# Keys and queries of a sparse-attention layer: projected by weights or by tokens

## The chip, the cores and the metric

The kernel runs on one core of a Trainium2 chip. The metric is the device time of one execution in microseconds; the lower the better. TensorE (PE) does matrix products into PSUM, VectorE (DVE), ScalarE (ACT) and GpSimd (POOL) do elementwise work, and SyncE (SP) issues the weight loads. Each engine carries out its own instructions strictly in the order in which they are written; semaphores tie the engines together.

## The reference, cut to what matters

A two-layer decoder trunk over 256 tokens of width 2048 in fp32. Layer 0 is stick-breaking attention and a gated MLP with a causal convolution. Layer 1 is a sparse attention, and again such an MLP. In layer 1 one weight matrix gives, per token, 16 query heads, 4 key heads, 4 value heads (each 128 wide) and an indexer whose top-k picks 64 keys per query:

```python
q = _rope(_rmsnorm(q, q_norm_g), cos, sin)      # 16 heads of 128
k = _rope(_rmsnorm(k, k_norm_g), cos, sin)      # 4 heads of 128
...
s = einsum(q, k of the selected positions) * attn_scale
p = softmax(s);  o = einsum(p, v);  x = x + o @ w_o
```

The norm is over the 128 values of a head; the rotation pairs value j with value j + 64. Four query heads share one key head and one value head.

## The kernel before, in words

**Weights.** All weights come as 771 "pieces" of 128 x 1024 fp32 through a ring of four buffers. For each piece SyncE loads `raw` (L240 to L251) as soon as VectorE is done with the piece four before it; ScalarE's `split` (L282, its instruction is L289) waits until PE has used the piece four before it (`piece_used`), and rounds the piece to `w_hi`; VectorE's `split` (L737, L747) forms `w_lo = raw - w_hi`. PE waits for `lo_ready`. Every other job of ScalarE and VectorE is written between the splits of certain pieces: the functions run over a slot number `e`, one per piece, and a job "at e" stands before or after the split of piece `e + 4`. This hand-written order is all that sets who does what when.

**Products.** The activations lie transposed as `xg[:, k, 0:256]` (high part) and `xg[:, k, 256:512]` (low part). `proj` (L1303) keeps a 128 x 128 tile of the weights stationary and streams activations: per tile one matmul of 512 columns with `w_hi` and one of 256 with `w_lo`, 16 matmuls and 6144 columns per piece; the result is channel by token, the high and low sums side by side. `proj_tokens` (L1352) keeps a 128 x 128 tile of the activations stationary and streams 512 weight columns: three matmuls of 512 columns for each of two row tiles and two token halves, 12 matmuls and 6144 columns per piece; the result is token by channel. Value heads already use it, as does the last product of layer 1 (with `hid` for `xg`).

**The stage of the change** is layer 1 after the value heads: blocks 9 and 10 (keys, two heads each, pieces `L1_K`), then blocks 11 to 18 (queries, two heads, a "pair", each, pieces `L1_Q`), four pieces a block, 40 pieces in all, then the output product `out_groups(BASE_WO[1], ...)` in four groups of eight pieces. Results of a block alternate between banks 0, 1 and 2, 3. After a block's last piece ScalarE copies one half of the sums (`evac`, L604), VectorE adds the other and scales (L1052), ScalarE squares, PE sums the squares over the channels with one fp32 matmul of 512 columns (`mean_squares`, L1582), ScalarE takes the root (`norm_scale`, L615), and VectorE rotates by three multiplications and two more passes (`rope`, L1072). Queries land in `qr`, keys in `k_all`.

**Attention of a pair t** runs one block later for the scores and two later for the rest, all in banks 6 and 7 with the output in bank 4: `scores` (L1608, fp32) on a mask that ScalarE seeded (L627); `maxes` and `normalise` on VectorE (L1161, L1169) around `exps` on ScalarE (L630) before the next block's first split; `transposes` (L1617) after the third piece of that block; `prt_copy` (L639), `values` (L1625) after its fourth; then `out_hi` and `out_lo` (L646, L1179). The last two pairs run among the first eight output pieces (`l1_head`, `l1_tail`). From `scores` to `transposes` of a pair PE has three pieces to do in between:

```python
if e == 2 and t_tr is not None:
    transposes(t_tr)
if e == 3:
    if t_tr is not None:
        values(t_tr, n_v)
    if t_score is not None:
        scores(t_score, g_score)
```

The top-k rounds on VectorE lie between the splits of the last value pieces and blocks 9 to 11, `select(1)` in block 11.

Of the kernel before, what the change touches and what calls it, by code (L numbers as in the profile page):

```python
# [26 lines left out]
P = 128  # L27
D = 2048
T = 256
# [33 lines left out]
L1_Q = L1_K + 8  # L63
BASE_WO = (QKV0, L1_Q + 4 * PAIRS)
# [7 lines left out]
NV = V_DSA + 3  # L72

C_TRI, C_ONE, C_AVG, C_ID, C_SBM, C_CM, C_COS, C_SIN = 0, 128, 256, 384, 512, 640, 1024, 1280
NC = 1536
# [6 lines left out]
def build(nc, x_in, w_all, vecs_in, consts_in, out):  # L82
    with ExitStack() as ctx:  # L83
# [47 lines left out]
        v_cur = sb("v_cur", [P, 2, P], F32, l1)  # L131
# [3 lines left out]
        usq = sb("usq", [P, 2, T], F32, l1)  # L135
        rsn = sb("rsn", [P, 2, T], F32, l1)
# [19 lines left out]
        rope_c = sb("rope_c", [P, 3, T], F32, l1)  # L156
        rope_s = sb("rope_s", [P, 3, T], F32, l1)
# [34 lines left out]
        v1_ready, vcur_ready = sem("v1_ready"), sem("vcur_ready")  # L192
# [18 lines left out]
        cos_t, sin_t = cst[:, C_COS:C_COS + T], cst[:, C_SIN:C_SIN + T]  # L211

# [15 lines left out]

        block = ctx.enter_context(nc.Block())
# [3 lines left out]
        def _(sp_q):  # L233
# [9 lines left out]
            sp_q.dma_start(avg_d[:, :], consts_in[:, NC:NC + P]).then_inc(avg_in, 16)  # L243
# [15 lines left out]
        def _(pool):  # L259
# [8 lines left out]
            for n in (2, 1, 0):  # L268
                pool.tensor_scalar(rope_c[:, n, :], cos_t, vecs[:, V_DSA + n:V_DSA + n + 1], None, ALU.mult)
                pool.tensor_scalar(rope_s[:, n, :], sin_t, vecs[:, V_DSA + n:V_DSA + n + 1], None, ALU.mult).then_inc(tables_ready, 1)  # L270
# [10 lines left out]
        def _(act):  # L281
# [152 lines left out]
            def l0_first():  # L434
                for e in range(12):
                    split(e + RING)
                    if e == 0:
                        act.dma_start(cst[:, :], consts_in[:, 0:NC]).then_inc(cst_in, 16)
                        act.dma_start(vecs[:, V_CONV:NV + 1], vecs_in[:, V_CONV:]).then_inc(vecs_in_s, 16)
# [156 lines left out]
            act.dma_start(cst[:, :], consts_in[:, 0:NC]).then_inc(cst_in, 16)  # L596
            def evac_index(B, bank0, last_piece):
                act.wait_ge(piece_used, last_piece + 1)
                if not (isinstance(B, int) and B == 0):
                    act.wait_ge(qr_ready, B)  # L600
                n = T - TI
                act.copy(tu[:, :, TI:T], psum[:, bank0:bank0 + 2, n:2 * n]).then_inc(rb_copied, 1)

            def evac(B, bank0, nh, last_piece, nb, u=tu, t_av=None):  # L604
                act.wait_ge(piece_used, last_piece + 1)
                if u is tu:
                    act.wait_ge(qr_ready, B)
                act.copy(u[:, 0:nh, :], psum[:, bank0:bank0 + nh, T:2 * T]).then_inc(rb_copied, 1)
                if t_av is not None:
                    out_hi(t_av)  # L610
                if nb is not None:
                    act.wait_ge(rb_u, nb + 1)
                    act.activation(usq[:, 0:nh, :], u[:, 0:nh, :], ACT.Square).then_inc(rb_sq, 1)

            def norm_scale(nh, nb):  # L615

                act.wait_ge(ms_ready, nb + 1)
                act.activation(rsn[:, 0:nh, :], psum[:, 5, 0:nh * T].rearrange("p (h t) -> p h t", h=nh), ACT.Ln, bias=eps_ap).then_inc(ln_ready, 1)
                act.wait_ge(ln_ready, nb + 1)
                act.activation(rsn[:, 0:nh, :], rsn[:, 0:nh, :], ACT.Exp, scale=-0.5).then_inc(rsn_ready, 1)  # L620
# [6 lines left out]
            def seed_scores():  # L627
                act.copy(psum[:, 6:8, 0:384], selm[:, :].unsqueeze(1).to_broadcast([P, 2, 384])).then_inc(s_seeded, 1)

            def exps(t):  # L630
                act.wait_ge(nm_ready, t + 1)
                for h in range(2):
                    for th in range(2):
                        c = slice(at[th], at[th] + width[th])
                        last = act.activation(pr[:, h, c], psum[:, 6 + h, c], ACT.Exp, bias=nmx[:, th, h:h + 1], scale=ATT_SCALE,
                                              accum_out=sums[:, th, h:h + 1])
                last.then_inc(p_ready, 1)

            def prt_copy(t):  # L639
                act.wait_ge(tr_ready, t + 1)  # L640
                act.copy(prt[:, :, :], psum[:, 6:8, 0:384]).then_inc(pt_ready, 1)
                if not isinstance(t, int) or t < PAIRS - 1:
                    act.wait_ge(pt_ready, t + 1)
                    seed_scores()

            def out_hi(t):  # L646
                act.wait_ge(av_ready, t + 1)
                act.copy(att[:, bass.ds(2 * t, 2), 0:T], psum[:, 4, :].rearrange("p (h t) -> p h t", h=2)).then_inc(att_hi, 1)

            def set_v(g):  # L650

                act.copy(v_cur[:, :, :], v_all[:, :, bass.ds(g * P, P)]).then_inc(vcur_ready, 1)
# [7 lines left out]
            for e in range(3):  # L660
# [4 lines left out]
                if e == 1:  # L665
                    evac(1, 2, 1, L1_KI + 1, 0, tki)
# [3 lines left out]
            def block1(B, i, per, par, nb, prev_norm, t_relu, t_soft, t_av, base, v_g=None, first_seed=False):  # L670


                for e in range(4):
                    if e == 0 and v_g is not None:
                        set_v(v_g)
                    if e == 0 and t_soft is not None:
                        exps(t_soft)
# [3 lines left out]
                    if e == 1 and prev_norm is not None:  # L681
                        norm_scale(prev_norm[1], prev_norm[0])
                    if e == 2 and t_soft is not None:
                        prt_copy(t_soft)
                    if e == 1 and first_seed:
                        act.wait_ge(rl_ready, PAIRS)
                        act.wait_ge(topk_s, TOPK_STEPS)
                        seed_scores()
                    if e == 3 and nb is None:
                        evac_index(B, 2 * par, base + times(i, per) + 3)  # L690
                    elif e == 3:
                        evac(B, 2 * par, 2, base + times(i, per) + 3, nb, t_av=t_av)

            block1(2, None, 0, 0, None, (0, 1), None, None, None, L1_QI)
            with act.Fori(0, 3) as i:
                block1(3 + 2 * i, i, 8, 1, None, None, 2 * i, None, None, L1_QI + 4)
                block1(4 + 2 * i, i, 8, 0, None, None, 2 * i + 1, None, None, L1_QI + 8)
# [8 lines left out]
            block1(9, None, 0, 0, 1, None, None, None, None, L1_K)  # L706
            block1(10, None, 0, 1, 2, (1, 2), None, None, None, L1_K + 4)
            block1(11, None, 0, 0, 3, (2, 2), None, None, None, L1_Q)
            block1(12, None, 0, 1, 4, (3, 2), None, None, None, L1_Q + 4, first_seed=True)
            with act.Fori(0, 3) as i:  # L710
                block1(13 + 2 * i, i, 8, 0, 5 + 2 * i, (4 + 2 * i, 2), None, 2 * i, 2 * i, L1_Q + 8, v_g=i)
                block1(14 + 2 * i, i, 8, 1, 6 + 2 * i, (5 + 2 * i, 2), None, 2 * i + 1, 2 * i + 1, L1_Q + 12)

            def l1_head(e):
                if e == 0:
                    set_v(3)
                    exps(6)
                if e == 3:
                    exps(7)

            def l1_tail(e):
                if e == 1:
# [1066 lines left out]
```

## Time and profile before

| | us |
|---|---|
| median of 3 runs | 2217.63 |
| lowest and highest | 2217.49, 2218.47 |
| span of the profiled execution, first to last instruction | 2216.0 |
| PE busy | 2209.4 |
| VectorE, ScalarE busy | 1484.4, 1177.3 |

The profiled execution is known by its span alone; the median of the timed runs is 1.6 us above that span. Busy times of one engine can overlap those of the others, so the table says which engine has no room left, not what each stage costs. A matmul's own duration reaches past the start of the next one; the pace of PE is read from starts.

### The profile page before, as it was taken

What the parts mean: (1) busy time and instruction counts of PE and PEld (TensorE: products, weight loads), DVE (VectorE), ACT (ScalarE), POOL (GpSimd) and SP (SyncE); (2) the same over time, 40 slices, a digit from 0 to 9 for tenths busy, and PEclk for the clock granted to TensorE, in tenths of its full rate; (3) what the DMA queues carried; (4) which work ended last, traced back from release to release, by engine and by line L of the source; (5) the groups of instructions that cost most, each with busy time, mean ns of one, the idle gap of its engine ahead of it and who ended that gap; (6) DMA issues with size and microseconds to landing.
All of it is one profiled execution on the core that took longest, in us unless ns stands there. A gap on an engine that the chain in (4) does not pass through costs nothing.

```text
span 2216.0 us, 34772 instructions
## 1 busy us (share of the span) xinstructions
PE 2209.4 (100%) x12470; PEld 1935.2 (87%) x12470; DVE 1484.4 (67%) x1753; ACT 1177.3 (53%) x1409; POOL 14.3 (1%) x21
## 2 busy tenths in 40 slices
PE   9999999999999999999999999999999999999999
PEld 8888898888888888888899888888888888888887
DVE  7666556677777777555578888667777777774443
ACT  7565555555555555444455466555555555553333
POOL 0000000000000000000010000000000000000000
PEclk9999999999999999999999999999999999999999
DMA  7555555555555555565566544555555656566664
GB/s 270 166 168 177 171 162 181 195 185 190 189 193 186 189 190 191 190 190 189 191 212 198 177 157 139 161 183 191 182 198 181 194 184 198 180 193 201 201 199 136
DMA packets 113829, 411.55 MB, mean 186 GB/s; under 512 B 12769, under 2 KB 13537, under 8 KB 113761
## 3 DMA queue, kind: packets, MB, share of 16 engines
q1 hardware_dynamic: 112320, 406.70, 56.5%
q10 hardware_dynamic: 1008, 2.30, 0.3%
q0 software_dynamic: 432, 1.57, 0.2%
q8 instruction: 51, 0.84, 0.2%
q14 instruction: 18, 0.14, 0.0%
HBM read 408.42 MB, written 2.10 MB: 185 GB/s over the span
## 4 chain that ended last, share of the span: by engine, by line
PE 99%; DMA 0%; SPq 0%; DVE 0%; ACT 0%; issue 0%; DVEq 0%
PE psum L1301 99%; DMA raw<-w_all 0%; PE psum L1621 0%; PE psum L1557 0%; DVE w_lo L747 0%; ACT w_hi L289 0%; SPq L237 0%; SPq L235 0%; DVE upad L822 0%; SPq L236 0%; SPq L234 0%; DVEq L83 0%
## 5 line engine op out<-in xcount | busy, mean ns | idle before, releaser
L747 DVE TENSOR_TENSOR w_lo<-raw,w_hi 128x1024 fp32r<-128x1024 f32 x769 | 935.6, 1224 | 678.6 <-ACT w_hi L289 672.8
L1301 PE MATMUL psum<-xg,w_hi 128*128 128x512 f32 (+1 forms) x3936 | 1358.3, 392 | 1.9 <-DVE w_lo L747 1.0
L289 ACT CAST w_hi<-raw 128x1024 fp32r<-128x1024 f32 x770 | 803.1, 1049 | 771.4 <-PE psum L1301 767.6
L1301 PE MATMUL psum<-xg,w_lo 128*128 128x256 f32 (+1 forms) x3920 | 1090.8, 278 | 0.0
L1301 PEld LDWEIGHTS psum<-xg,w_hi 128*128 128x128 f32 x3936 | 736.0, 187 | 156.7 <-issue 2.2
L1301 PEld LDWEIGHTS psum<-xg,w_lo 128*128 128x128 f32 x3920 | 742.6, 189 | 2.6 <-issue 2.2
L1301 PE MATMUL psum<-hid,w_hi 128*128 128x512 f32 x704 | 244.1, 391 | 0.0
L1301 PE MATMUL psum<-w_hi,hid 128*128 128x512 f32 x704 | 217.9, 390 | 0.0
L1301 PE MATMUL psum<-hid,w_lo 128*128 128x256 f32 x704 | 197.4, 280 | 0.0
L1301 PE MATMUL psum<-att,w_hi 128*128 128x512 f32 x512 | 178.8, 393 | 0.0
L1301 PEld LDWEIGHTS psum<-hid,w_hi 128*128 128x128 f32 x704 | 131.7, 187 | 28.6
L1301 PEld LDWEIGHTS psum<-w_hi,hid 128*128 128x128 f32 x704 | 132.2, 188 | 27.3
L1010 DVE SCALAR_TENSOR_TENSOR conv<-upad,vecs,conv 128x256 f32<-128x256 f32 x352 | 147.1, 480 | 6.4
L1301 PE MATMUL psum<-att,w_lo 128*128 128x256 f32 x512 | 143.5, 280 | 0.0
L1301 PE MATMUL psum<-w_lo,hid 128*128 128x512 f32 x352 | 137.0, 389 | 0.0
L1301 PEld LDWEIGHTS psum<-hid,w_lo 128*128 128x128 f32 x704 | 133.4, 189 | 0.0
L548 ACT ACTIVATE conv<-upad,vecs 128x256 f32<-128x256 f32 x176 | 91.6, 591 | 46.9 <-DVE upad L1005 46.9
L1301 PEld LDWEIGHTS psum<-att,w_hi 128*128 128x128 f32 x512 | 95.8, 187 | 20.7
L1301 PE MATMUL psum<-w_hi,xg 128*128 128x512 f32 (+1 forms) x384 | 105.5, 357 | 0.0
L1301 PEld LDWEIGHTS psum<-att,w_lo 128*128 128x128 f32 x512 | 97.0, 189 | 0.1
L1301 PEld LDWEIGHTS psum<-w_lo,hid 128*128 128x128 f32 x352 | 66.1, 188 | 13.5
L1301 PEld LDWEIGHTS psum<-w_hi,xg 128*128 128x128 f32 x384 | 68.3, 189 | 9.9
(176 smaller groups left out, 1062.9 us busy)
## 6 DMA issues: line engine op xcount, KB each, us to landing
raw<-w_all SPq DMA_DIRECT2D x770, 512.0 KB, 3.8
xres<-x_in SPq DMA_DIRECT2D x3, 512.0 KB, 9.0
cst<-consts_in ACTq DMA_DIRECT2D x2, 768.0 KB, 6.6
raw<-w_all SPq DMA_DIRECT2D x2, 256.0 KB, 3.6
xres<-x_in SPq DMA_DIRECT2D x2, 256.0 KB, 3.8
out_t<-part POOLq DMA_DIRECT2D x1, 512.0 KB, 7.3
out_t<-conv POOLq DMA_DIRECT2D x1, 512.0 KB, 7.4
out_t<-gates POOLq DMA_DIRECT2D x1, 512.0 KB, 7.0
```

The lines of the kernel that those rows point to most:

```text
L289: act.copy(w_hi[:, c % RING, :], raw[:, c % RING, :]).then_inc(hi_ready, 1)
L548: last = act.activation(conv[:, k, :], upad[:, k, 0:T], ACT.Identity, scale=conv_scalars(layer, i, val, k, 0), bias=conv_scalars(layer, i, ...
L747: dve.tensor_tensor(w_lo[:, c % RING, :], raw[:, c % RING, :], f32(w_hi[:, c % RING, :]), ALU.subtract).then_inc(lo_ready, 1)
L1010: last = dve.scalar_tensor_tensor(out=conv[:, k, :], in0=upad[:, k, j:j + T], scalar=conv_scalars(layer, i, val, k, j), in1=conv[:, k, :], ...
L1301: return pe.matmul(o, lhsT, rhs, start=start, stop=True, skip_group_check=True)
```

## The change

Keys and queries are projected with `proj_tokens`, four heads (512 columns, eight pieces) at once: a "quad". There are five quads: n = 0 is the keys, n = 1 to 4 the queries. Quad n uses banks 0, 1 or 2, 3. The 40 pieces and their bytes stay, laid out as 512 columns. The head norm is by token: ScalarE copies the two banks (`copy_tokens`) and squares eight times 128 x 128 with a running sum (`square_tokens`); small operations of 128 x 8 make the scale `tsc`. The rotation is by token (`rope_tokens`). For keys the scale is multiplied in; for queries it goes into the exponential. Then PE turns heads by products with the identity: eight transposes of 128 x 128 for the keys, eight per quad of queries. The fp32 matmuls of `mean_squares` are left out for these heads. The attention of a pair is unchanged in its matmuls but takes banks 4, 5 or 6, 7 by turns, and its output stays in its own bank. It is written once per quad of two pairs a, b, by slots of the following quad (the last one by slots of the first eight output pieces). The loops over three block pairs are written out.

PE, new:

```diff
+            def turn_queries(t):
+                pe.wait_ge(tok_roped, t // 2 + 2)
+                if t > 1:
+                    pe.wait_ge(att_ready, PAIRS + t - 1)
...
+            def attend(e, g):
+                a, b = 2 * g, 2 * g + 1
+                if e == 1:
+                    turn_queries(a)
+                    turn_queries(b)
+                if e == 2:
+                    scores(a)
+                if e == 3:
+                    scores(b)
+                    transposes(a)
+                if e == 4:
+                    values(a)
+
+            def attend_midway(e, g):
+                if e == 5:
+                    transposes(2 * g + 1)
+                if e == 6:
+                    values(2 * g + 1)
...
+            for n in range(QUADS):
...
+                for e in range(8):
+                    mid = (lambda: attend_midway(e, n - 2)) if n > 1 else None
+                    proj_tokens(L1_K + 8 * n + e, None, 0, ((psum[:, b, :], True), (psum[:, b + 1, :], True)), 2, 2 * e, 512, e == 0, mid)
+                    if n == 1 and e == 4:
+                        turn_keys()
+                    if n > 1:
+                        attend(e, n - 2)
...
             def wo1_ready(e):
                 if e == 0:
-                    pe.wait_ge(rb_sum, 18)
+                    pe.wait_ge(tok_copied, 2 * QUADS - 2)
                 pe.wait_ge(att_ready, PAIRS + e + 1)
-                return (rb_sum, 19) if e == 0 else None
+                return (tok_copied, 2 * QUADS) if e == 0 else None
```

`attend_midway` is called in the middle of a piece. In the first output piece column tiles 2, 3 now come before 0, 1, and the second wait of `wo1_ready` stands before tile 0.

ScalarE, new:

```diff
+            def copy_tokens(n):
+                act.wait_ge(piece_used, L1_K + 8 * n + 8)
...
+                for th in range(2):
+                    act.copy(raw_tok[:, th, :], psum[:, quad_bank(n) + th, :]).then_inc(tok_copied, 1)
...
+            def copy_queries(t):
+                act.wait_ge(tq_ready, t + 1)
...
+                act.copy(qd[:, t % 2, :, :], psum[:, b, :].rearrange("p (h t) -> p h t", h=2)).then_inc(qd_ready, 1)
...
+                act.copy(psum[:, b:b + 2, 0:384], selm[:, :].unsqueeze(1).to_broadcast([P, 2, 384])).then_inc(s_seeded, 1)
...
+            def attend_before(e, g):
+                a, b = 2 * g, 2 * g + 1
+                if e == 0:
+                    root_tokens(g + 1)
+                if e == 3:
+                    exps(a)
+                if e == 4:
+                    prt_copy(a)
+                    exps(b)
+                if e == 5:
+                    out_hi(a)
+                if e == 6:
+                    prt_copy(b)
+                if e == 7:
+                    out_hi(b)
+
+            def attend_after(e, g):
+                if e == 1:
+                    copy_queries(2 * g)
+                    copy_queries(2 * g + 1)
...
+                    split(L1_K + 8 * n + e + RING)
+                    if n > 1:
+                        attend_after(e, n - 2)
+                    if e == 7:
+                        copy_tokens(n)
+                        square_tokens(n)
```

VectorE, new (`attend_before` stands before the split of its slot, `rope_tokens` after that of slot 7):

```diff
+            def rope_tokens(n):
+                dve.wait_ge(tok_copied, 2 * n + 2)
...
+                for th in range(2):
...
+                    dve.tensor_tensor(rot4[:, th, :, :], raw4[:, th, :, :], c_t, ALU.mult)
+                    for to, fr in ((0, half), (half, 0)):
...
+                        last = dve.tensor_tensor(sin4[:, th, :, to:to + half], raw4[:, th, :, fr:fr + half], s_t, ALU.mult)
...
+                dve.tensor_tensor(rot_tok, rot_tok, sin_tok, ALU.add).then_inc(tok_roped, 1)
...
+            def attend_before(e, g):
+                a, b = 2 * g, 2 * g + 1
+                if e == 0:
+                    mean_tokens(g + 1)
+                if e == 1:
+                    scale_tokens(g + 1)
+                if e == 3:
+                    maxes(a)
+                    normalise(a)
+                if e == 4:
+                    maxes(b)
+                    normalise(b)
+                if e == 5:
+                    out_lo(a)
+                if e == 7:
+                    out_lo(b)
```

Beside that: ScalarE's queue loads a further table of 128 x 512 (`cst_tok`, 256 KB) at the start of layer 1, right behind the 768 KB of `cst`; in layer 0 `cst` loads 640 columns in place of 1536 and `vecs` 256 more. GpSimd makes token tables by six multiplications in place of four of the six before. VectorE gets two operations on 128 x 2 after `recip(2)`. `select(1)` moves to slot 4 of quad 1.

## Rows read from the trace of the kernel before

**Rows 1.** The page: busy time, granted clock by slices, chain by engine.

```profile
PE 2209.4 (100%) x12470; PEld 1935.2 (87%) x12470; DVE 1484.4 (67%) x1753; ACT 1177.3 (53%) x1409; POOL 14.3 (1%) x21
...
PEclk9999999999999999999999999999999999999999
...
PE 99%; DMA 0%; SPq 0%; DVE 0%; ACT 0%; issue 0%; DVEq 0%
```

**Rows 2.** Timeline of PE, the changed stage: start, us, what.

```profile
1244.70 0.39 PE L1301 MATMUL psum<-xg,w_hi 128*128 128x512 f32 x1
...
1261.66 1.02 PE L1301 MATMUL psum<-usq,cst 128*128 128x512 f32 x2
...
1262.86 0.40 PE L1301 MATMUL psum<-xg,w_hi 128*128 128x512 f32 x1
...
1273.61 1.02 PE L1301 MATMUL psum<-usq,cst 128*128 128x512 f32 x2
...
1274.71 0.28 PE L1301 MATMUL psum<-xg,w_lo 128*128 128x256 f32 x1
...
1413.29 0.39 PE L1301 MATMUL psum<-att,w_hi 128*128 128x512 f32 x1
```

**Rows 3.** Chain that ended last, in order: start, us, what.

```profile
1969.70 0.88 PE psum L1557 x8
1970.57 59.90 PE psum L1301 x264
```

**Rows 4.** Timelines of PE and ScalarE at one piece's end.

```profile
1236.32 0.61 PE L1301 MATMUL psum<-w_hi,xg 128*128 128x512 f32 x2
...
1236.80 1.05 ACT L289 CAST w_hi<-raw 128x1024 fp32r<-128x1024 f32 x1 [2.01 <-PE psum L1301]
```

**Rows 5.** Timeline of ScalarE, one block of query heads.

```profile
1297.10 0.37 ACT L635 ACTIVATE pr<-psum,nmx 128x128 f32<-128x128 f32 x1 [0.21 <-DVE nmx L1167]
...
1297.46 0.47 ACT L635 ACTIVATE pr<-psum,nmx 128x256 f32<-128x256 f32 x1
...
1298.61 0.21 ACT L635 ACTIVATION_READ_ACCUMULATOR pr<-psum,nmx 128x1 f32 x1
...
1304.55 0.80 ACT L628 COPY psum<-selm 128x768 f32<-128x768 f32 x1
...
1307.15 0.58 ACT L608 COPY tu<-psum 128x512 f32<-128x512 f32 x1
1307.63 0.59 ACT L648 CAST att<-psum 128x512 f32 x1
```

**Rows 6.** Timeline of VectorE, one block of query heads.

```profile
1295.84 1.01 DVE L1164 TENSOR_REDUCE mx<-psum 128x2 f32<-128x256 f32 x2
...
1299.06 1.01 DVE L1176 TENSOR_SCALAR pr<-pr,rc 128x128 f32<-128x128 f32 x4
1299.99 2.36 DVE L747 TENSOR_TENSOR w_lo<-raw,w_hi 128x1024 fp32r<-128x1024 f32 x2
1302.26 0.69 DVE L1076 TENSOR_TENSOR ra<-tu,rope_c 128x512 f32<-128x512 f32 x1
1302.96 1.39 DVE L1079 TENSOR_TENSOR rb<-tu,rope_s 64x512 f32<-64x512 f32 x2
```

**Rows 7.** Groups of VectorE by form: busy us, mean ns, idle before.

```profile
L778 DVE TENSOR_TENSOR gates<-gates,conv 128x1024 f32<-128x1024 f32 x1 | 1.2, 1219 | 0.0
...
L1079 DVE TENSOR_TENSOR rb<-tki,rope_s 64x256 f32<-64x256 f32 x2 | 0.8, 420 | 0.0
```

**Rows 8.** Timelines of ScalarE and GpSimd, start of layer 1.

```profile
1136.96 2.95 ACT L289 CAST w_hi<-raw 128x1024 fp32r<-128x1024 f32 x3 [0.23 <-DMA cst<-consts_in]
...
1147.60 0.31 POOL L272 MEMSET ones<- 128x256 f32 x1
```

**Rows 9.** Timeline of PE after its wait near the start.

```profile
10.86 0.50 PE L1301 MATMUL psum<-xg,w_hi 128*128 128x512 f32 x1 [1.01 <-DVE w_lo L747]
11.20 0.28 PE L1301 MATMUL psum<-xg,w_lo 128*128 128x256 f32 x1
```

More of the change, by code:

```diff
@@ L211, in build @@
         cos_t, sin_t = cst[:, C_COS:C_COS + T], cst[:, C_SIN:C_SIN + T]
+        cos_tok, sin_tok_t = cst_tok[:, 0, :, :], cst_tok[:, 1, :, :]
         z_all = psum[:, 5:7, :].rearrange("p b c -> p (b c)")[:, 0:ZN]
@@ L1310, in proj @@
                 s = c % RING
-                for ct in range(cols // P):
-                    if ct == 2 and upper_free is not None:
-                        pe.wait_ge(*upper_free)
+                tiles = range(cols // P) if freed is None else (2, 3, 0, 1)
+                for ct in tiles:
+                    if ct == 0 and freed is not None:
+                        pe.wait_ge(*freed)
+                    if ct == 2 and midway is not None:
+                        midway()
                     for kk in range(kts):
@@ L1357, in proj_tokens @@
                     w = slice(kk * cols, (kk + 1) * cols)
+                    if kk == 1 and midway is not None:
+                        midway()
                     for th in range(2):
@@ L1620, in transposes, with values @@
                     for c in range(3):
-                        last = pe.matmul(psum[:, 6 + h, c * P:(c + 1) * P], pr[:, h, c * P:(c + 1) * P], ident, start=c == 0, stop=True,
+                        last = pe.matmul(psum[:, pair_bank(t) + h, c * P:(c + 1) * P], pr[:, h, c * P:(c + 1) * P], ident, start=c == 0, stop=True,
                                          is_transpose=True, skip_group_check=True)
                 last.then_inc(tr_ready, 1)
-            def values(t, n_v):
+            def values(t):
@@ new lines, in attend_midway, with block1 @@
+            def attend_midway(e, g):
[3 more added lines that the diff above has]
+                    values(2 * g + 1)
+            def block1(B, i, per, par, first, t_log, base):
+                pe.wait_ge(rb_sum, B - 1)
+                for e in range(4):
+                    proj_index(base + e, i, per, 2 * par, 4 * e, e == 0)
+                    if e == 1 and first:
+                        mean_squares()
+                    if e == 2 and first:
+                        turn_wi()
+                    if e == 3 and t_log is not None:
+                        logits(t_log)
```

506 lines of the change are left out of this document (257 added, 249 removed).

## The prediction

> **What bounds the kernel now.** I read the page first: PE is busy for 2209.4 of 2216.0 us, its granted clock is full in all 40 slices, and the chain that ended last is 99% PE [rows 1]. So the time is the sum of PE's own work, and the change counts in two ways: what PE has to do, and whether PE must now wait. For the work I took PE's timeline over the changed stage [rows 2] and the merged chain for whole pieces [rows 3]. For the waits I took the ScalarE and VectorE jobs that will stand between two PE jobs, from their timelines [rows 4 to 6]. The stage, from the first key piece to the end of the eighth output piece, is 1413.29 - 1244.70 = 168.6 us [rows 2].
>
> **PE's work.** Pieces: 22 token pieces take 59.90 us, 2.72 each [rows 3]. With the weights stationary, 31 pairs of matmuls start within 1273.61 - 1262.86 = 10.75 us, 0.347 a pair, 2.77 a piece of eight pairs [rows 2]. 40 pieces save 40 x 0.05 = 2.0 us. The six pieces from 1244.70 to 1261.66 ran slower, 0.353 a pair, which gives 0.3 more [rows 2]. A rule of the Trainium skill speaks here, TensorE: Matmul & The Clock Gate, section "Wait — 56ns, not 53.3ns?": start to start is columns over clock plus about 2.5 ns a matmul. By it four matmuls fewer a piece save 0.01 us, 0.4 us in all in place of 2.0. The rows are measured in this kernel, so they decide.
>
> Ten mean squares go. One delays the next low-part matmul to 1274.71 - 1273.61 = 1.10 us [rows 2], less the 0.23 of an ordinary 512-column matmul (2.72 / 12), so 0.87 each, 8.7 in all. Forty identity products come; eight take 0.88 us [rows 3], so 4.4 in all. Scores, values and probability transposes are as many as before. Sum: -2.0 - 0.3 - 8.7 + 4.4 = **-6.6 us**, if nothing waits.
>
> **The waits.** Call T the moment at which PE could start the piece after a quad's last. PE runs two pieces, to T + 5.44, and then wants `turn_queries`. Four waits follow per quad.
>
> (a) Turning. ScalarE sees the last piece at T + 0.25 (1236.32 plus one slot of 0.23, against 1236.80) [rows 4]. It splits first; splits are (2.95 - 1.05) / 2 = 0.95 apart [rows 8]. Two copies, 0.48 apart and 0.58 long [rows 5], end at T + 2.26. VectorE gets the split at T + 1.33, is free 1.14 later (two take 2.36) [rows 6], at T + 2.47, and rotates: 0.70 for 512 elements, going by the spacing of the two rows at 1302.26 and 1302.96 [rows 6], and 0.42 for each of two halves of 256 [rows 7], twice, so 3.08, or 2.6 if neighbours overlap by 0.09 as its splits do. The addition of 1024 is 1.22 [rows 7]. With 0.04 between dependent jobs it is done at T + 6.3 to T + 6.8. I take 6.65: PE waits **1.2 us**.
>
> (b) Scores of a. ScalarE's root waits for `mean_tokens`, which stands behind the rotation on VectorE: 6.7. Two small functions (the nearest rows have 0.21 and 0.37 [rows 5], I take 0.27) end at 7.3. Then come, in its order, two splits (9.2), the copy of pair a (9.8) and the seed, 0.80 [rows 5], done at 10.65. PE has turned two pairs by 6.65 + 0.88 and used a piece by 10.25: **0.4 us**. The eight squares, 0.36 apart (1297.10 to 1297.46) [rows 5], end at 5.3, behind the cover of the rotation.
>
> (c) Transposes of a, the largest. Before, three pieces lie between scores and transposes, 8.3 us. Now it is one piece and the scores of b: 2.72 + 1.30 (768 fp32 columns by the 0.87 for 512). The scores of a start at T + 10.7 and are seen at 12.15. But ScalarE is still at copy and seed of pair b until 11.9, then splits (12.95), VectorE splits too (14.1), and only then come maxima and their negation. From the first maximum to the last normalised probability the chain took 1300.07 - 1295.84 = 4.23 [rows 6], the exponentials in it 1298.82 - 1297.10 = 1.72 [rows 5]. That ends at 18.4. PE is there at 10.7 + 1.3 + 2.72 + 1.3 = 16.0: **2.4 us**. Were both engines free when the scores end, 0.5 would be left.
>
> (d) Values of b. `prt_copy` of b stands behind a split that waits for piece 5 to be used: 0.25 + 0.95 + 0.80 + 0.05 = 2.05 after that piece. PE is there after half a piece, 1.36: **0.7 us**.
>
> That is 4.7 us per quad, three times, 14.1. In the output stage the first piece also waits for the copies of the last quad (2.3 against 1.4 for two tiles: 0.9), which leaves (a) 0.2; (b) to (d) are 0.4, 2.4 and 0.7. Last, output piece 7 needs the output of pair 7, whose values now come in the middle of piece 6, where a whole piece lay between: split seen by VectorE at 0.25 + 1.08, 1.14 for it, 0.69 for `out_lo` (as the 512-wide row), 0.05: 3.2 us. Sum 7.8. Each of the 18 restarts costs PE some more: after a wait of 1.01 us the next matmul starts 0.34 later in place of 0.23 [rows 9], 0.1 each, 1.8 us.
>
> **Costed at nothing.** Rotation and squares drop from VectorE and ScalarE elsewhere in the stage, but neither bounds it; no credit. GpSimd's tables were done at 1147.60 [rows 8], over 100 us ahead of first use; its work could double unseen, and if it were late the first rotation would wait. The 256 KB of `cst_tok` share the DMAs with `cst`, for which ScalarE waited 0.23 us [rows 8]; at the rate at which PE uses up 512 KB pieces (2.77 us each) that is 0 to 1.4 us later, covered by the ring of four pieces; uncovered it would cost 1.4. Two operations on 128 x 2 on VectorE are behind the same ring; as dear as the 0.42 of 256 elements, they would cost 0.8 uncovered. The smaller loads in layer 0 run beside PE; 0. `select(1)` is needed a quad later; a ring piece covers its 2.6 us.
>
> **Sum.** -6.6 + 14.1 + 7.8 + 1.8 = **+17.1 us**. The rows are of an execution with a span of 2216.0, 1.6 below the median of 2217.6; on the median the forecast is **2234.7 us**.
>
> **Rivals.** (1) *The work alone counts.* Total waits stay under 6.6 us, because the chains behind the turns and transposes are shorter than I add them up: faster, down to 2217.6 - 6.6 = 2211.0. It decides at 1.5 us a quad. For it: VectorE has less to do, 67% busy already [rows 1]. Against: order, not load, makes these waits, and 4.23 us do not fit into 4.0. Chance 0.07. (2) *Only the bare chains count.* VectorE and ScalarE are free when the scores end, and (c) falls to 0.5: 2234.7 - 4 x 1.9 = 2227. Chance 0.14. (3) *The clock falls.* PE ran at full clock throughout with almost no idle time [rows 1]; after the 1.0 us wait near the start its pace was full at once [rows 9], which speaks against it. But gaps of 2.4 and 3.2 us occur in no row. If after each of the five the next piece ran at 1.2 GHz, 5 x 2.72 = 13.6 us come on top: 2248. The Trainium skill, TensorE: Matmul & The Clock Gate, section "HAM oscillation — how this bites in real kernels", says that idle gaps between matmuls put the clock back to half; no row here shows it. Chance 0.07. (4) *Gain and waits cancel* within 0.2% (4.4 us, about what a measurement of this kernel can tell from no change): 0.05. The forecast keeps 0.67.
>
> **Range.** Low end: rival (2), the rotation at its lower bound (4 x 0.5 less) and restarts free (1.8): 2223. High end: halves of the rotation as dear as whole ones (0.28 x 4 x 4 = 4.5), restarts at 0.2 (1.8), `cst_tok` uncovered (1.4): 2242. Faster 0.07, same 0.05, slower 0.88.
>
> **What would show it.** PE's list of waits, almost empty before, should name VectorE's normalised probabilities as the largest entry, some 2.4 us four times, then `rot_tok`, the seeds, `prt` and once `att` with 3.2. PE's share should fall to 99%, with some 22 us idle. Token pieces should run at 2.72 and eight turns take 0.88; the stage of 168.6 should last 186. Waits under 1.5 us a quad would make the forecast wrong, and so would a granted clock below full.

## The result and the profile after

The changed kernel takes 2237.41 us (median of 4 runs, 2236.29 to 2238.28) against 2217.70 before: a ratio of 1.0087, 95% interval 1.0075 to 1.0099. It is 19.7 us slower; the forecast of 2234.7 was 2.7 us too low, inside its range. The time lies wholly in the stage of the change: from key piece 0 (1245.22, the second matmul of its row) to output piece 8 (1433.51) it lasts 188.3 us, against 168.6 [rows 2]. The forecast had 186 for it.

The page of the kernel after (busy time, slices, chain), beside [rows 1]:

```profile
PE 2212.8 (99%) x12330; PEld 1929.2 (86%) x12330; DVE 1459.7 (65%) x1730; ACT 1181.9 (53%) x1482; POOL 16.4 (1%) x23
...
PE   9999999999999999999999998899999999999999
...
PE 95%; DVE 2%; ACT 2%; issue 1%; DMA 0%; SPq 0%; DVEq 0%; ACTq 0%
```

PE has 140 matmuls fewer and is busy for longer all the same. Two slices show it partly idle, and DVE and ACT are now on the chain that ended last, with 2% each, where they had nothing.

PE's list of waits in the kernel after (us in total, times, longest):

```profile
PE psum L1749 <- DVE pr L1283: 9.5, 4, 2.4
PE psum L1399 <- DVE att L1289: 3.0, 1, 3.0
PE psum L1731 <- DVE conv L1192: 2.5, 3, 0.8
PE psum L1399 <- ACT prt L728: 2.1, 4, 0.5
PE psum L1399 <- POOL part L290: 1.3, 1, 1.3
PE psum L1399 <- ACT part L667: 0.8, 1, 0.8
PE psum L1399 <- DVE w_lo L829: 0.5, 1, 0.5
PE psum L1399 <- DVE xg L840: 0.3, 1, 0.3
PE psum L1399 <- ACT psum L711: 0.2, 1, 0.2
```

Six of these nine are the ones that the prediction named: the probabilities before `transposes(a)`, the output of pair 7, the turned heads (`rot_tok` lies in the buffer `conv`), `prt`, the copies of the last quad (`part`) and a seed (`psum`). Together they are 18.1 us. The other three lie in the first 11 us of the kernel.

The second quad of queries, PE's timeline of the kernel after (start, us, what, in brackets the idle time before and its releaser):

```profile
1339.81 1.47 PE L1399 MATMUL psum<-k_all,qd 128*128 128x128 f32 x8
1343.65 0.88 PE L1749 MATMUL psum<-cst,pr 128*128 128x128 f32 x6 [2.37 <-DVE pr L1283]
1344.29 0.48 PE L1399 MATMUL psum<-w_hi,xg 128*128 128x512 f32 x1
```

And ScalarE and VectorE before the first such wait, the kernel after, beside [rows 5, 6]:

```profile
1300.49 0.80 ACT L711 COPY psum<-selm 128x768 f32<-128x768 f32 x1
1301.22 1.04 ACT L326 CAST w_hi<-raw 128x1024 fp32r<-128x1024 f32 x1
1304.69 0.46 ACT L719 ACTIVATE pr<-psum,nmx,tsc 128x128 f32<-128x128 f32 x1 [2.42 <-DVE nmx L1273]
...
1305.14 0.55 ACT L719 ACTIVATE pr<-psum,nmx,tsc 128x256 f32<-128x256 f32 x1
```

```profile
1302.30 1.22 DVE L829 TENSOR_TENSOR w_lo<-raw,w_hi 128x1024 fp32r<-128x1024 f32 x1 [2.21 <-ACT w_hi L326]
1303.44 1.01 DVE L1268 TENSOR_REDUCE mx<-psum 128x2 f32<-128x256 f32 x2
...
1306.80 0.18 DVE L1278 RECIPROCAL rc<-sums 128x4 f32<-128x4 f32 x1 [2.15 <-ACT pr L719]
1307.01 1.01 DVE L1283 TENSOR_SCALAR pr<-pr,rc 128x128 f32<-128x128 f32 x4
```

It is the order of the prediction's (c): copies and seeds hold ScalarE until 1301.3, its split follows, then VectorE's, and only then come maxima, exponentials and normalisation, 1303.44 to 1308.0. Both engines stand idle for over 2 us in between, each waiting for the other.

What the prediction had as a rival shows here as well. PE's timeline after two of its five long waits, kernel after:

```profile
1308.08 1.54 PE L1749 MATMUL psum<-cst,pr 128*128 128x128 f32 x6 [2.38 <-DVE pr L1283]
1309.27 0.78 PE L1399 MATMUL psum<-w_hi,xg 128*128 128x512 f32 x1
...
1428.22 0.80 PE L1399 MATMUL psum<-att,w_hi 128*128 128x512 f32 x1 [3.05 <-DVE att L1289]
...
1429.03 0.63 PE L1399 MATMUL psum<-att,w_hi 128*128 128x512 f32 x1
...
1433.51 0.63 PE L1399 MATMUL psum<-att,w_hi 128*128 128x512 f32 x1
```

The six transposes at 1308.08 take 1.19 us start to start, the same six at 1343.65 take 0.64; the pairs of output piece 7 are 0.64 apart ((1433.51 - 1429.03) / 7) where 0.347 is full pace [rows 2]. The windows view of the same kernel puts the granted clock beside it (window, length, busy PE, PEld, DVE, ACT, POOL, then PEclk, DMA share, GB/s):

```profile
1308.00:1312.00 4.00, 3.92 (x14) 3.42 (x15) 2.25 (x5) 2.35 (x8) 0.00 (x0) 0.60 0.35 131
1340.00:1345.00 5.00, 2.63 (x17) 2.09 (x17) 2.78 (x10) 3.45 (x10) 0.00 (x0) 1.00 0.32 111
...
1408.00:1414.00 6.00, 3.64 (x24) 3.01 (x23) 3.75 (x11) 3.81 (x10) 0.00 (x0) 1.00 0.27 89
1426.00:1436.00 10.00, 7.78 (x29) 6.70 (x30) 2.94 (x3) 2.75 (x4) 0.00 (x0) 0.66 0.18 54
```

So TensorE's clock went to its lower level, 1.2 GHz, after the first and the last of the five long waits (2.38 and 3.05 us), and stayed at 2.4 GHz after the three between them, of 2.36 to 2.37 us (the left-out stretch from 1374 has 1.00 too). It cost about 1.4 us the first time (0.55 on the transposes, the rest on the products behind them, up to 1311.12): from the transposes to the next turns it is 23.64 us in this quad (1331.72 - 1308.08) and 22.20 in the next (1365.85 - 1343.65). The second time it cost about 2.7 (nine pairs, to 1434.13, at 0.64 for 0.347).

### The profile page after: what moved, and what is told of

Its sections match the earlier page's. It is cut to its first block, busy times and chain, and to the rows that moved or that the text cites. A ratio compares the mean times of both kernels' runs of the same rounds, so it can differ in the third digit from the quotient of the medians.

```text
span 2236.5 us, 34380 instructions
## 1 busy us (share of the span) xinstructions
PE 2212.8 (99%) x12330; PEld 1929.2 (86%) x12330; DVE 1459.7 (65%) x1730; ACT 1181.9 (53%) x1482; POOL 16.4 (1%) x23
## 4 chain that ended last, share of the span: by engine, by line
PE 95%; DVE 2%; ACT 2%; issue 1%; DMA 0%; SPq 0%; DVEq 0%; ACTq 0%
PE psum L1399 95%; ACT w_hi L326 1%; ACT pr L719 0%; PE psum L1749 0%; DVE w_lo L829 0%; DMA raw<-w_all 0%; ACT qd L707 0%; DVE mx L1268 0%; DVE pr L1283 0%; DVE gates L1189 0%; DVE conv L1186 0%; DVE conv L1192 0%; PE psum L1661 0%; ACT prt L728 0%; DVE xg L840 0%
## 5 line engine op out<-in xcount | busy, mean ns | idle before, releaser
L1399 PE MATMUL psum<-xg,w_hi 128*128 128x512 f32 (+1 forms) x3616 | 1241.2, 390 | 0.9 <-DVE w_lo L829 0.5
L1399 PE MATMUL psum<-xg,w_lo 128*128 128x256 f32 (+1 forms) x3600 | 1000.0, 278 | 0.0
L1399 PEld LDWEIGHTS psum<-xg,w_hi 128*128 128x128 f32 x3616 | 675.8, 187 | 141.6 <-DVE w_lo L829 1.0
L1399 PEld LDWEIGHTS psum<-xg,w_lo 128*128 128x128 f32 x3600 | 680.7, 189 | 0.4
L1399 PE MATMUL psum<-w_hi,xg 128*128 128x512 f32 (+1 forms) x704 | 210.8, 377 | 0.0
L1399 PEld LDWEIGHTS psum<-w_hi,xg 128*128 128x128 f32 x704 | 128.8, 189 | 22.4
L1399 PE MATMUL psum<-w_lo,xg 128*128 128x512 f32 (+1 forms) x352 | 130.5, 371 | 0.0
```

Of the source, the lines that this page charges most:

```text
L1399: return pe.matmul(o, lhsT, rhs, start=start, stop=True, skip_group_check=True)
```

## The experiments

The theory: PE waits because each link from PE over ScalarE and VectorE back to PE now has one piece or half a piece of cover, and the hand-written order puts splits, copies and seeds between its parts; the work itself is about 6 us cheaper. Rival A: the new form costs PE more by itself (identity products, restarts, pace). Rival B: the lower clock is the larger part. The medians, all beside runs of the kernel before (2217.7 to 2218.1 in each group), and the length of the stage in the profiled execution of each kernel:

| kernel | median us (range) | ratio to before, 95% | stage, us |
|---|---|---|---|
| changed | 2237.41 (2236.29-2238.28) | 1.0087 (1.0075-1.0099) | 188.3 |
| changed, repeated | 2237.66 (2235.04-2239.16) | 1.0086 (1.0072-1.0099) | 187.6 |
| output of pair 7 earlier | 2232.67 (2231.52-2234.47) | 1.0070 (1.0053-1.0086) | 181.4 |
| last wait filled | 2234.72 (2233.75-2236.61) | 1.0075 (1.0058-1.0092) | 185.9 |
| copies and rotation first | 2235.57 (2233.73-2238.55) | 1.0077 (1.0060-1.0094) | 186.8 |
| constant scale | 2236.17 (2235.37-2238.22) | 1.0085 (1.0069-1.0101) | 187.0 |
| four waits filled | 2236.35 (2235.07-2236.96) | 1.0082 (1.0066-1.0098) | 184.9 |
| four waits filled, shorter | 2235.83 (2234.79-2237.28) | 1.0079 (1.0065-1.0093) | 186.1 |
| quads in later slots | 2221.49 (2218.72-2222.98) | 1.0017 (1.0008-1.0027) | 170.0 |
| all reordered | 2213.60 (2212.06-2214.38) | 0.9980 (0.9971-0.9990) | 163.2 |
| all reordered, turns twice | 2217.60 (2216.22-2218.41) | 0.9998 (0.9989-1.0008) | 166.6 |

### The output of pair 7 one slot earlier

```diff
 ScalarE, attend_before:            VectorE, attend_before: the same for out_lo(b)
-                if e == 7:
+                if e == (6 if g == KVH - 1 else 7):
                     out_hi(b)
```

> In the output stage the two halves of the last pair's output (ScalarE's out_hi, VectorE's out_lo) move from before the split of slot 7 to before the split of slot 6; nothing else changes. Theory, that the place in the order makes the wait: the 3.05 us wait before output piece 7 shrinks to about 0.2 us, and the 18 matmuls at half clock behind it (5.9 us for what takes 3.1) go too: 2237.4 - 2.9 - 2.8 = 2231.7 us. Rival, that the copies themselves are too slow for PE whatever their place: the wait stays, no change.

Measured: 2232.67. The wait for `att` is gone from the list of waits; those for `pr`, `conv` and `prt` stay at 9.5, 2.5 and 2.1. The stage is 6.9 us shorter. The wait is 3.05 of that and the lower clock behind it some 2.7; the rest comes from another place, for in this execution the clock did not fall after the first long wait either, though that wait was the same (PE's timeline):

```profile
1306.90 0.87 PE L1749 MATMUL psum<-cst,pr 128*128 128x128 f32 x6 [2.39 <-DVE pr L1283]
```

The row has 0.87 where the changed kernel had 1.54. The median moved by 4.7, 1.0 less than the wait and the lower clock of output piece 7 together; the profiled execution, at a mean clock of 1.000, is the fastest of the four, and the other three have 0.999. One slot in the order is worth 4.7 us.

### The last wait filled with idle products

```diff
+                if e == 7:
+                    for n in range(8):
+                        mm(psum[:, 4, 0:T], xg[:, 0, 0:P], xg[:, 1, 0:T], True)
+                        mm(psum[:, 4, 0:P], xg[:, 0, 0:P], xg[:, 1, 0:P], True)
                 pe.wait_ge(att_ready, PAIRS + e + 1)
```

> Eight pairs of matmuls of 256 and 128 columns into an unused bank (results never read) are put in front of PE's wait before output piece 7; the wait itself stays. Theory, that idleness of PE makes the clock fall: the granted clock stays full after the wait and 2.8 us are gained although work is added: 2234.6 us. Rival, that the clock fell for another reason, or that the slow matmuls behind the wait are its restart: no gain, 2237.4 or a little more.

Measured: 2234.72. `att` is as late as before, but output piece 7 now runs at full pace behind a remaining wait of 1.26 (PE's timeline):

```profile
1427.65 0.50 PE L1399 MATMUL psum<-att,w_hi 128*128 128x512 f32 x1 [1.26 <-DVE att L1289]
...
1428.10 0.40 PE L1399 MATMUL psum<-att,w_hi 128*128 128x512 f32 x1
```

Pairs are 0.35 apart ((1430.58 - 1428.10) / 7), and the stage is 2.4 us shorter, near the 2.7 that the lower clock cost there. The fall after the first wait was still there in this execution.

### Copies and rotation ahead of the split

```diff
+                    if e == 7:
+                        copy_tokens(n)
                     split(L1_K + 8 * n + e + RING)
...
                     if e == 7:
-                        copy_tokens(n)
                         square_tokens(n)
 VectorE: rope_tokens(n), mean_tokens(n) likewise ahead of the split of slot 7
```

> At a quad's last slot ScalarE copies the two banks before its split in place of after it, and VectorE rotates and takes the mean before its split. Theory: the wait before the turns (0.8 us idle, three times) and the 0.8 us before tiles 0, 1 of the first output piece vanish; but the waits before the transposes stay, since they hang on the seeds and splits behind the turn; everything starts earlier by up to 1 us, so the gain may be taken once per quad only: 3.3 to 4 us, 2233.5 us. Rival, that the turns wait for VectorE's load and not its order: no change.

Measured: 2235.57, a gain of 1.8 where 3.9 was expected: half a miss. The waits went as expected: `conv`, `part` and the seed are gone from the list, 3.5 us, and the others stay (9.4, 3.0, 2.1). But in this execution the clock fell after four waits, three of them ones that the changed kernel passed at full clock (PE's timeline, the third long wait):

```profile
1374.61 1.37 PE L1747 MATMUL psum<-cst,pr 128*128 128x128 f32 x6 [2.39 <-DVE pr L1284]
```

The mean granted clock of its four runs is 0.996 to 0.998, against 0.998 to 0.999 of the changed kernel. So the clock took back a part of what the order gave. Why it fell more often here is not shown.

### The scale of the exponentials as a constant

```diff
-  act.activation(pr[...], psum[...], ACT.Exp, bias=nmx[...], scale=tsc[:, th, j + h:j + h + 1], ...)
+  act.activation(pr[...], psum[...], ACT.Exp, bias=nmx[...], scale=ATT_SCALE, ...)
```

`nmx` is then the maximum times the negative constant; this leaves out the norm of the query heads.

> The changed kernel with a constant scale in the exponentials and in the negated maxima, as before the change; it leaves out the query heads' norm. Theory: the scale read per partition makes the four exponentials of a pair 2.07 us in place of 1.72, and this lies in the chain scores to transposes, so the wait before the transposes falls by 0.35 us four times, the one before the values of b not: 2237.4 - 1.4 = 2236.0 us (the clock's falls scatter by as much; the profile's waits decide: 2.0 in place of 2.4 us). Rival, that the longer exponentials lie beside other work: waits unchanged at 2.4.

Measured: 2236.17, and the exponentials are back at the length of [rows 5] (ScalarE's timeline):

```profile
1303.90 0.37 ACT L719 ACTIVATE pr<-psum,nmx 128x128 f32<-128x128 f32 x1 [2.43 <-DVE nmx L1273]
...
1304.26 0.46 ACT L719 ACTIVATE pr<-psum,nmx 128x256 f32<-128x256 f32 x1
```

The waits before the transposes fall from 9.5 to 8.1 in total, 2.0 each, as expected. The difference is the column `tsc` as scale: 0.46 and 0.55 us against 0.37 and 0.46; the step that makes `nmx` takes 0.16 and 0.17. Here the clock fell after the fourth and the fifth of the long waits (2.00 and 3.05 us) and not after the first.

### Four waits filled

```diff
+            def fill(bank, n):
+                for _ in range(n):
+                    mm(psum[:, bank, 0:T], xg[:, 0, 0:P], xg[:, 1, 0:T], True)
+                    mm(psum[:, bank, 0:P], xg[:, 0, 0:P], xg[:, 1, 0:P], True)
...
                     scores(b)
+                    if g < KVH - 1:
+                        fill(quad_bank(g + 1), 12)
                     transposes(a)
...
+                if e == 7:
+                    fill(4, 12)
```

> Twelve pairs of matmuls (256 and 128 columns, results never read) in front of the wait before the transposes of a in quads 2 to 4 and before the wait for output piece 7; all waits end when they did. Theory, that the clock falls only after long idle stretches and that this is a part of the loss: full clock in the stage, waits seen as under 0.8 us, 2237.4 - 4.3 = 2233.1 us although PE does more, and a smaller scatter. Rival, the clock falls anyway or does not matter: 2237 or more.

Measured: 2236.35, a miss by 3.3 us in the median. The stage did get 3.4 us shorter, at full clock throughout. The 24 products of a fill last 2.90 us, though, and run past the probabilities, so that the transposes start 4.02 after the scores where it was 3.84 (PE's timeline):

```profile
1340.65 1.47 PE L1399 MATMUL psum<-k_all,qd 128*128 128x128 f32 x8
1341.77 3.07 PE L1399 MATMUL psum<-xg 128*128 128x256 f32 x24
1344.67 0.83 PE L1754 MATMUL psum<-cst,pr 128*128 128x128 f32 x6
```

And this execution lost 2.2 us before the stage, at its start, by a wait of 2.52 us for `xg` (0.28 in the changed kernel) with the lower clock behind it:

```profile
9.68 0.76 PE L1399 MATMUL psum<-xg,w_hi 128*128 128x512 f32 x1 [2.52 <-DVE xg L840]
```

That start is common to all kernels here, and its wait differs from execution to execution (0.28, 1.0, 1.4, 2.52 us): a scatter that is no effect of any edit. The turns of the keys, ahead of which PE has the same work in every kernel since the change, start at 1282.75 here and between 1279.40 and 1280.77 in the ten other profiled executions. So differences of one or two us between medians of four runs say little, and the length of the stage says more.

### The same with shorter fills, and the changed kernel again

```diff
-                        fill(quad_bank(g + 1), 12)
+                        fill(quad_bank(g + 1), 10)
```

> The changed kernel once more, beside the next one on the same chip, since its four runs spread over 2 us. Both theories: 2237.4, within 1 us. If TensorE's clock falls after the 3 us gap in every execution, the mean clock of each run is 0.998 to 0.999, never 1.000.

> As the filled kernel before, but 10 pairs in place of 12 before the first transposes of each of three quads, so that the fill (24 matmuls took 2.91 us, so 20 take 2.42) ends 0.3 us before the probabilities are there rather than 0.2 us after. Theory: the clock costs the changed kernel about 1.5 us after the first 2.4 us gap and 2.4 us before output piece 7, and the overrun cost the last fill 3 x 0.2; without overrun the time is 3.9 below the changed kernel, 2233.5, and the mean clock is 1.000 where the start has no long wait. Rival: the falls are there only in profiled executions or are made up elsewhere, and fills gain nothing: 2236.5 to 2237.4.

Measured: 2237.66 for the changed kernel, with falls after the same two waits (the last one shorter: a granted clock of 0.83 from 1426 to 1436, where it was 0.66), and a mean clock of 0.998 to 0.999 in each of the five runs. The filled kernel took 2235.83, 2.3 us over what was expected. The windows view of it, same stretches as above:

```profile
1408.00:1414.00 6.00, 3.63 (x14) 3.23 (x14) 3.41 (x9) 4.12 (x14) 0.00 (x0) 0.72 0.33 117
1426.00:1436.00 10.00, 9.67 (x61) 8.53 (x60) 5.21 (x5) 3.89 (x5) 0.00 (x0) 1.00 0.26 84
```

The falls at 1308 (clock 1.00 there) and at 1426 are gone, and one came at 1410, after the only long wait left unfilled, where the changed kernel had kept its clock. Runs with a mean clock of 1.000 took 2234.79 to 2235.83 and those with 0.999 took 2236.74 and 2237.28. By the stage the longer fills bought 3.4 us and the shorter ones 2.2, with one fall left. That filling sends the fall on to the next wait is not shown: the kernel with longer fills passed the same unfilled wait (2.32 us) at full clock, and the one with the constant scale fell there with nothing filled. Rival B is bounded: the clock is worth about 4 us of the 19.7, and the kernel with the earlier output, in the run whose trace shows no fall at all and with one wait less, is still 13.8 us behind (2231.52 against 2217.7).

### Quads in later slots

PE turns after slot 2, scores after slots 3 and 4, transposes of a after 5, values of a in the middle of 6, transposes of b in the middle of 7, values of b in slot 0 of the next quad; ScalarE and VectorE follow. The output stage stays as in the changed kernel.

```diff
-                if e == 1:
+                if e == 2:
                     turn_queries(a)
                     turn_queries(b)
-                if e == 2:
+                if e == 3:
                     scores(a)
-                if e == 3:
+                if e == 4:
                     scores(b)
+                if e == 5:
                     transposes(a)
-                if e == 4:
-                    values(a)
...
+                if e == 0 and g:
+                    values(a - 1)
...
+                if e == 6:
+                    values(a)
+                if e == 7:
+                    transposes(b)
```

> Only for the attention written into query quads 2 to 4: turns after slot 2, scores after 3 and 4, transposes of a after 5, values of a in the middle of 6, transposes of b in the middle of 7, values of b after slot 0 of the next quad, with the jobs of ScalarE and VectorE moved along; the output stage keeps its slots. Same instructions, same number. Theory: the four waits of each of the three quads vanish (4.2 to 4.7 us each, 13) and the half clock behind the first of them too (1.5): 2237.4 - 14.3 = 2223 us, and the stage from key piece 0 to output piece 8 shrinks from 188.3 to 174 us. Rival, that VectorE and ScalarE cannot keep up with attention at all in this form: waits move to other slots, over 2232 us.

Measured: 2221.49. Of the stage's waits only those of the output stage are left, the fourth being 0.5 for `prt` (list of waits):

```profile
PE psum L1432 <- DVE att L1304: 3.0, 1, 3.0
PE psum L1782 <- DVE pr L1298: 1.8, 1, 1.8
...
PE psum L1432 <- ACT part L667: 0.8, 1, 0.8
```

Not a matmul was removed, and 15.9 us came back. This separates theory and rival A: the order is the loss, not the form. In this execution even the 3.05 us wait for `att` left the clock at full. It is the fastest of ten, 2.8 us under the median, and most of the others have a mean clock of 0.999.

### All reordered

To this it adds copies and rotation ahead of the split, and the output stage in new slots: scores of b after 3, transposes of a in the middle of 4 and values of a after it, transposes of b after 5, values of b in the middle of 6 with its output right behind, and VectorE's maxima of a already in slot 2.

```diff
                 if g == KVH - 1:
...
                     if e == 3:
                         scores(b)
-                        transposes(a)
                     if e == 4:
                         values(a)
+                    if e == 5:
+                        transposes(b)
                     return
...
                 if g == KVH - 1:
-                    if e == 5:
-                        transposes(b)
+                    if e == 4:
+                        transposes(a)
                     if e == 6:
                         values(b)
```

> The new slots in query quads 2 to 4, the copies and the rotation ahead of the splits of a quad's last slot, and for the output stage: turns after slot 1, scores after 2 and 3, transposes of a in the middle of 4, values of a after 4, transposes of b after 5, values of b in the middle of 6, both output halves before the splits of slot 6. Same instructions and number as the changed kernel. Theory, that the change's work alone is -6.6 us and all the rest is order: no PE wait over 0.5 us in the stage, full clock, stage from key piece 0 to output piece 8 at 162 us, 2217.8 - 6.6 + 0.5 = 2211.7 us, faster than both. Rival, that part of the loss is in the pieces or products themselves (token pieces dearer between fp32 jobs, turns dearer than 0.11 us): stage over 165 us with no waits, 2215 us or more.

Measured: 2213.60 in 11 runs, 4.2 us under the kernel before (ratio 0.9980, 0.9971 to 0.9990). Its whole list of PE's waits is that of the kernel's start:

```profile
PE psum L1429 <- POOL part L290: 1.3, 1, 1.3
PE psum L1429 <- DVE xg L855: 1.1, 2, 0.6
```

PE's timeline of this kernel, from behind the turns of the keys to those of the second quad of queries:

```profile
1280.42 0.48 PE L1429 MATMUL psum<-w_hi,xg 128*128 128x512 f32 x1
...
1296.85 1.04 PE L1761 MATMUL psum<-cst,conv 128*128 128x128 f32 x8
...
1326.39 1.04 PE L1761 MATMUL psum<-cst,conv 128*128 128x128 f32 x8
```

A quad takes 29.54 us (1326.39 - 1296.85) against 34.13 in the changed kernel. The stage is 163.2 us, 5.4 under that before: this is the change's work on PE by itself, which the prediction put at -6.6.

### The same with every query head turned twice

```diff
-                for h in range(2):
+                for h in (0, 1, 0, 1):
```

> The version of the run beside it with each of the 32 identity products of the query turns done twice, same result. Theory, that PE's work is all that counts once the waits are gone: 32 x 0.11 = 3.5 us more than that run, some 2215.2 us. Rival, that turns hide behind something: no difference.

Measured: 2217.60, 4.0 more for 32 more products, 0.5 over what was expected; the stage is 3.4 longer, as expected. The period of a quad in PE's timeline tells it best: 1327.73 - 1297.31 = 30.42, so 0.88 for eight, 0.11 each.

```profile
1297.31 0.93 PE L1761 MATMUL psum<-cst,conv 128*128 128x128 f32 x7
...
1327.73 1.25 PE L1761 MATMUL psum<-cst,conv 128*128 128x128 f32 x10
```

## Why the prediction was right, and where its sizes were off

**The work.** Forecast -6.6, measured -5.4 in the stage without waits. Identity products cost 0.11 each, as taken. Token pieces with nothing between them cost what I took: 13 of them start between the first key piece and the turns of the keys, (1280.59 - 1245.22) / 13 = 2.72 us each. The step that was too large is the saving where fp32 products stand between the pieces. PE's timelines of the kernel before and of the kernel after:

```profile
1302.58 0.82 PE L1621 MATMUL psum<-cst,pr 128*128 128x128 f32 x6
...
1378.90 0.82 PE L1621 MATMUL psum<-cst,pr 128*128 128x128 f32 x6
```

```profile
1244.99 0.62 PE L1399 MATMUL psum<-w_hi,xg 128*128 128x512 f32 x2
...
1280.59 1.04 PE L1715 MATMUL psum<-cst,conv 128*128 128x128 f32 x8
```

Before, five pairs take 76.32 us, so two take 30.53; the reordered quad takes 29.54. That is 0.99 less, where my terms give 8 x 0.05 + 2 x 0.87 - 0.88 = 1.26. Three such quads are 0.8 of the missing 1.2; the other 0.4 is open. Token pieces right behind fp32 products take 2.84 to 2.97 us, which no term had. Behind the turns of the keys, 72 matmuls take 1296.85 - 1280.42 = 16.43 us, 2.74 a piece, with the slower start in them. The Trainium skill, TensorE: Matmul & The Clock Gate, section "Wait — 56ns, not 53.3ns?", gives by its 2.5 ns a matmul an estimate of 0.4 us saved over all 40 pieces; the plain pieces, 2.72 against 2.77, do not bear it out.

**(a) Turning.** Forecast 1.2 in each of three quads, measured 0.82; in the output stage 0.2 forecast, none. The 2.6 of my two bounds was the right one: cosine and sine products and the addition start at 1292.14, 1292.74, 1293.41, 1294.02 and 1294.80, 2.66 us in all. I took 3.08. The squares came 0.29 apart, not 0.36, and hid as said.

```profile
1292.14 0.68 DVE L1186 TENSOR_TENSOR conv<-part,tok_c 128x512 f32<-128x512 f32 x1
...
1294.80 1.23 DVE L1192 TENSOR_TENSOR conv<-conv,gates 128x1024 f32<-128x1024 f32 x1
```

**(b) Scores of a.** Forecast 0.4 four times, measured 0.16 once. With the rotation done earlier, the seed was too. The scores themselves take 1.12 us (1301.61 - 1300.49, reordered kernel); I had 1.30.

**(c) Transposes of a.** Forecast 2.4 four times, measured 2.37 four times. The argument that the splits of both engines stand between scores and maxima is what the rows show. Two errors in it cancelled: the root, its splits and the seeds came earlier than I had them, since the rotation did, and the exponentials took 2.07 us (1304.69 to 1306.76) where I took 1.72 from rows with a constant scale. The constant scale shows the second: 8.1 in place of 9.5. So the mechanism was right and the closeness of the number is in part luck. Rival (2), bare chains, needs 0.5 here and fell.

**(d) Values of b.** Forecast 0.7 four times, measured 0.53. **Output stage:** `part` 0.76 for 0.9, `att` 3.05 for 3.2. All six kinds of waits: 18.1 measured, 21.9 forecast.

**Restarts.** Forecast 0.1 each, too low. From the scores to the transposes PE takes 1343.65 - 1339.81 = 3.84 us, where 1.12 without a wait (1301.61 - 1300.49 in the reordered kernel); that is 2.72 for 2.37 of idle, 0.35 more. The view counts a wait from the end of the row before it, and the scores' row is 1.47 long where the next matmul can start after 1.12: the same 0.35. Ahead of the turns it is 0.16: the last matmul of the piece starts at 1294.88 and the turns at 1296.09, 1.21 us for a usual 0.23 and 0.82 of idle. So the loss goes with what stands before the wait, and idle time in the list understates each wait by it. Sum for the stage: 18.1 - 5.4 + 4.1 for the clock leaves 2.9 for 14 restarts, against the 1.8 of the forecast; four behind the scores and ten behind other matmuls make 4 x 0.35 + 10 x 0.16 = 3.0.

**The clock.** Rival (3) priced five falls at 2.72 each and had a chance of 0.07. It came true by a third: two falls, 1.4 and 2.7 us. I had argued from a wait of 1.0 us that a gap does nothing [rows 9], and behind its first matmul the kernel before had no longer one; this step failed, and the forecast had the clock at nothing. The section "HAM oscillation — how this bites in real kernels" of the same page of the Trainium skill says that idle gaps put the clock back to half. The trace agrees for two long waits of five, not for three of 2.36 to 2.37 us; the views read here do not show what decides between them.

**How near the number is.** Four terms were off: clock +4.1, work +1.2, restarts +1.1, waits -3.8. Together they are +2.6, which takes the forecast +17.1 to the measured +19.7. That the waits, taken too long, made up for the clock, left out, is luck. The prediction also said that a granted clock below full would make it wrong; the clock did fall, twice, and the time stayed inside the range all the same, since the waits were shorter than forecast and two falls cost 4.1 us, not the 13.6 of rival (3).

**Rivals (1) and (4)** fell with the waits: they needed under 1.5 us a quad, and a quad had 0.82 + 2.37 + 0.53 = 3.7. But the reordered kernel reaches 2213.6, near rival (1)'s 2211.0: the work alone does count once nothing waits. **Costed at nothing** were the tables, the extra loads and `select(1)`: no wait for any of them is in PE's list.

## What to carry to other kernels

Where order is written by hand, a chain that leaves the bounding engine and comes back needs cover of its own length; count the chain with every split, copy and seed that stands in front of its links, not its links alone. When a change saves work on the bounding engine and the time rises, move the dependent steps before giving it up: here the same instructions in other slots turned +19.7 us into -4.2. Gaps of 2 to 3 us on TensorE may cost more than their length, here 1.4 to 2.7 us more when the clock fell, so price one with and without a fall.

## What the runs showed of the hardware that was not expected

- The clock fell to 1.2 GHz after some waits of 2.0 to 2.4 us and kept 2.4 GHz after others of the same length, in one execution and between executions. Counting the four waits before the transposes and then the one of 3.05 us for `att`, it fell in the changed kernel after the first and the fifth, with copies first after all but the first, with the constant scale after the fourth and the fifth, with shorter fills after the fourth, with the earlier output after none. In the kernel with quads in later slots it did not fall after the 3.05 us either. What decides is not shown by these views.
- An exponential whose scale is a column per partition takes 0.09 us longer than one with a constant (0.46 against 0.37 for 128 elements, 0.55 against 0.46 for 256).
- A wait costs PE more than the idle time in the list, at full clock: 0.35 us more behind the scores, 0.16 behind an ordinary 512-column matmul. It is the part of the last row that usually lies over the next matmul.
- Behind a wait filled with idle products the clock stayed up in every profiled execution here: behind the last wait in three kernels, behind the first three in two. Each pair of them took 0.24 us (2.90 / 12), so a fill longer than the wait took back part of what it gave. By the stage the longer fills gave 3.4 us, about what the two falls cost less the overrun (4.1 - 3 x 0.2); the median shows less (1.1 us), and the start of the kernel scatters by more than that.
